# Making the last chunk of five output blocks in the middle of the sixth block's chunks

## The reference

```python
z = h @ w_in                                   # h = modulated rmsnorm(x)
att = neighbourhood attention(q, k, v, context keys and values)   # 512 features
sg, cv = gated parts of z                                         # 256 + 256 features
y = concat([att, sg, cv]) @ w_out              # 1024 x 1024, the first output product
x = x + mod[2] * y                             # mod: six vectors of c @ ada_w + ada_b
h2 = rmsnorm(x, norm2_g) * (1 + mod[4]) + mod[3]
x = x + mod[5] * conv_ffn(h2)
```

## Time and profile before

| | |
|---|---|
| median of 3 runs | 1409.8 us (1407.17 to 1410.17) |
| the profiled execution's own time | 1409.92 us |
| its span | 1408.6 us |
| TensorE busy (matmuls) | 1365.2 us, 97% of the span |
| VectorE busy | 757.5 us, 54% |
| ScalarE busy | 605.3 us, 43% |
| mean granted clock of TensorE | 0.990 |

### The profile page before, as it was taken

How to read it: one execution, slowest core, us unless ns; L and a number is a source line. 1 busy time by engine, 2 the same in 40 slices (tenths; PEclk the granted TensorE clock), 3 DMA queues, 4 the chain that set the end, 5 groups by cost and what they waited for, 6 DMA issues and landing times.

```text
span 1408.6 us, 17387 instructions
## 1 busy us (share of the span) xinstructions
PE 1365.2 (97%) x7040; PEld 1129.4 (80%) x7040; DVE 757.5 (54%) x1070; ACT 605.3 (43%) x866; POOL 4.0 (0%) x11
## 2 busy tenths in 40 slices
PE   5999997999999999999999999999999999999997
PEld 4777776788888888888888888788997888888887
DVE  5678855575555443335524444345777666564224
ACT  5646866453333333223334545334524443443221
POOL 0000000000000000000000000000000000000000
PEclk9999999999999999999999999999999999999999
DMA  9743321323432323323232121234402323323331
GB/s 379 279 140 136 124 72 59 127 76 135 149 135 90 105 86 98 95 82 104 70 110 71 64 75 45 76 95 143 137 1 77 103 90 105 104 86 98 95 95 60
DMA packets 43102, 150.45 MB, mean 107 GB/s; under 512 B 4752, under 2 KB 6928, under 8 KB 41872
## 3 DMA queue, kind: packets, MB, share of 16 engines
q1 hardware_dynamic: 42144, 144.76, 31.1%
q0 software_dynamic: 880, 4.59, 1.0%
HBM read 146.45 MB, written 2.10 MB: 105 GB/s over the span
## 4 chain that ended last, share of the span: by engine, by line
PE 88%; DVE 6%; ACT 3%; issue 2%; DMA 1%; DVEq 0%; SPq 0%; ACTq 0%
PE banks L578 26%; PE banks L579 26%; PE banks L580 26%; ACT w_hi L1315 1%; PE banks L719 1%; DVE w_lo L1864 1%; PE banks L730 1%; PE banks L722 1%; PE banks L1125 1%; PE banks L1124 1%; PE banks L863 1%; PE banks L1116 1%; PE banks L1152 1%; PE banks L846 1%; PE banks L692 1%
## 5 line engine op out<-in xcount | busy, mean ns | idle before, releaser
L578 PE MATMUL banks<-h_lo,w_hi 128*128 128x512 f32 (+1 forms) x1248 | 475.3, 381 | 6.7 <-DVE h_lo L2203 2.1
L579 PE MATMUL banks<-h_hi,w_lo 128*128 128x512 f32 (+1 forms) x1248 | 471.5, 378 | 0.0
L580 PE MATMUL banks<-h_hi,w_hi 128*128 128x512 f32 (+1 forms) x1248 | 470.0, 377 | 0.0
L1864 DVE TENSOR_TENSOR w_lo<-raw_w,w_hi 128x1024 fp32r<-128x1024 f32 (+2 forms) x221 | 256.1, 1161 | 323.9 <-ACT w_hi L1315 321.6
L1315 ACT ACTIVATE w_hi<-raw_w 128x1024 fp32r<-128x1024 f32 (+2 forms) x221 | 221.6, 1005 | 236.8 <-PE banks L580 210.6
L578 PEld LDWEIGHTS banks<-h_lo,w_hi 128*128 128x128 f32 x1248 | 236.2, 189 | 58.5 <-issue 7.4
L580 PEld LDWEIGHTS banks<-h_hi,w_hi 128*128 128x128 f32 x1248 | 236.2, 189 | 43.5
L579 PEld LDWEIGHTS banks<-h_hi,w_lo 128*128 128x128 f32 x1248 | 236.4, 189 | 41.7
L578 PE MATMUL banks<-a_lo,w_hi 128*128 128x512 f32 (+1 forms) x396 | 146.2, 369 | 0.0
L579 PE MATMUL banks<-a_hi,w_lo 128*128 128x512 f32 (+1 forms) x396 | 146.2, 369 | 0.0
L580 PE MATMUL banks<-a_hi,w_hi 128*128 128x512 f32 (+1 forms) x396 | 145.3, 367 | 0.0
(11 more groups left out here) (314 smaller groups left out, 1517.9 us busy)
## 6 DMA issues: line engine op xcount, KB each, us to landing
raw_w<-in_w_ffn_up SPq DMA_DIRECT2D x44, 512.0 KB, 3.3
raw_w<-in_w_up SPq DMA_DIRECT2D x44, 512.0 KB, 3.4
raw_w<-in_ada_rows SPq DMA_DIRECT2D x24, 512.0 KB, 4.0
early<-in_ada_turned SPq DMA_DIRECT2D x8, 1024.0 KB, 17.2
raw_w<-in_w_gates SPq DMA_DIRECT2D x16, 512.0 KB, 3.3
raw_w<-in_w_ffn_down SPq DMA_DIRECT2D x16, 448.0 KB, 3.3
raw_w<-in_w_down SPq DMA_DIRECT2D x16, 448.0 KB, 3.4
raw_w<-in_w_conv SPq DMA_DIRECT2D x12, 512.0 KB, 3.2
```

What stands on the lines that cost most here:

```text
L578: e.matmul(dst, lhs_hi, rhs_lo, start=first, stop=False)
L579: e.matmul(dst, lhs_lo, rhs_hi, start=False, stop=False)
L580: return e.matmul(dst, lhs_hi, rhs_hi, start=False, stop=last)
L1864: e.tensor_tensor(lo[:, 0:n], raw[:, i % RAW, 0:n], hi[:, 0:n].bitcast(F32), ALU.subtract).then_inc(s_lo, 1)
```

## The change

Four things are done. (1) The tile "last" is loaded before "full0", so "last" is tile 25 and "full0" tile 26. (2) TensorE makes four chunks of block 5, then the eighth chunk of blocks 0 to 4, then the last four chunks of block 5. `freed[0]` is now given after them, and the count in it is 11, since block 5 is added into x last. (3) VectorE adds blocks 0 to 4 first and block 5 after them; the sums of squares lag by one block. The split of "full1"'s first tile, which VectorE did as the last thing of output block 4 in the mixer, is done after `attended_lo`; rows 22 and 23 of `ada_w` are asked for in the step of block 3. (4) `modulation_ready(3, 2)` and the vector `gain` stand ahead of the additions instead of behind them. ScalarE's squares follow the new order of blocks.

```diff
--- before.py
+++ after.py
@@ -132,10 +132,10 @@
     for o in range(OUT_SPLIT):
         l.tile("out", io["w_out"][o, :, 0:KC - 1, :], (KC - 1) * P, 0, KC - 1)
         l.row()
+    l.tile("last", io["w_out_last"][:, :], OUT_SPLIT * P, 0, OUT_SPLIT)
     l.block("full0", "w_out", OUT_SPLIT)
     while l.n_rows < ROWS_BEFORE_NORM2:
         l.row()
-    l.tile("last", io["w_out_last"][:, :], OUT_SPLIT * P, 0, OUT_SPLIT)
     for o in range(OUT_SPLIT + 1, KC):
         l.block("full1", "w_out", o)
     for f in range(FC):
@@ -532,7 +532,7 @@
         HALF = T // 2
         HALVES = [slice(0, HALF), slice(HALF, T)]
         NT = TT // 2
-        FINAL_ORDER = (OUT_SPLIT, *range(OUT_SPLIT))
+        FULL_BEFORE_LAST = 4
         ADA_BANKS = (4, 5, 4, NORM_BANKS[0])
         LATE_BANKS = (1, 2, 3, 4, 5)
         LAST_TWO = (OUT_SPLIT + 1, OUT_SPLIT + 2)
@@ -947,16 +947,19 @@
 
 
 
-            for j in range(KC):
+            for j in range(FULL_BEFORE_LAST):
                 out_product(OUT_SPLIT, W["full0"], j, 0, KC)
-            freed[0] = (s_x1, OUT_SPLIT + 1)
             for o in range(OUT_SPLIT):
                 hi, lo = tile_of(W["last"])
                 b, w, k = LATE_BANKS[o], slice(o * P, (o + 1) * P), OUT_ORDER[KC - 1]
                 free(b)
+                e.wait_ge(s_mix_lo, KC)
                 done = product(bank[b][:, :], hi[:, w], lo[:, w], h_hi[:, k, :], h_lo[:, k, :], True, True)
                 done.then_inc(s_late if o < OUT_SPLIT - 1 else s_used, 1)
-                freed[b] = (s_x1, OUT_SPLIT + 2 + o)
+                freed[b] = (s_x1, OUT_SPLIT + 1 + o)
+            for j in range(FULL_BEFORE_LAST, KC):
+                out_product(OUT_SPLIT, W["full0"], j, 0, KC)
+            freed[0] = (s_x1, 2 * OUT_SPLIT + 1)
 
             def second_sum(half):
                 b, tok = NORM_BANKS[half], HALVES[half]
@@ -1559,11 +1562,11 @@
                 e.activation(h_hi[:, k, HALVES[half]], piece(half, k), ACT.Identity,
                              bias=mod[:, 3 * KC + k:3 * KC + k + 1]).then_inc(h_two.hi.sem, 1)
 
-            prepare(W["full0"] + 3)
+            prepare(W["last"] + 3)
             e.preload_act_table(ACT.Sqrt)
-            for n, o in enumerate(FINAL_ORDER):
-                x1_square(n, OUT_SPLIT + n + 1, x[:, o, :], squares[:, (n - 1) % 2, :] if n else exact[:, 0, :])
-                if n == 0:
+            for o in range(OUT_SPLIT + 1):
+                x1_square(o, OUT_SPLIT + o + 1, x[:, o, :], squares[:, (o - 1) % 2, :] if o else exact[:, 0, :])
+                if o == 1:
                     prepare(W["full1"] + 2)
             prepare(W["up"] + 1)
             for n, o in enumerate(LAST_TWO):
@@ -2165,7 +2168,10 @@
                         e.wait_ge(s_mod, 1)
                         e.wait_ge(s_used, t + 1)
                         add_gated(b, o, 2 * KC, s_x1)
-                        after_tile(t)
+                        if o < OUT_SPLIT - 1:
+                            after_tile(t)
+                        if o == OUT_SPLIT - 2:
+                            rows(loads.tile_load[W["full1"]])
 
 
 
@@ -2204,9 +2210,11 @@
                                        in1=h_hi[:, k, tok].bitcast(F32), op0=ALU.add, op1=ALU.subtract).then_inc(h_two.lo.sem, 1)
 
             every = slice(0, T)
-            e.wait_ge(s_used, W["full0"] + 1)
-            add_gated(0, OUT_SPLIT, 2 * KC, s_x1, every)
             low(W["full1"] + 1)
+            modulation_ready(3, 2)
+            e.wait_ge(s_mod, 2)
+            e.scalar_tensor_tensor(out=gain[:, :], in0=mod[:, 4 * KC:5 * KC], scalar=1.0, in1=cols_of("norm2_g"), op0=ALU.add,
+                                   op1=ALU.mult).then_inc(s_mod, 1)
             for o in range(OUT_SPLIT):
                 if o < OUT_SPLIT - 1:
                     e.wait_ge(s_late, o + 1)
@@ -2214,15 +2222,14 @@
                     e.wait_ge(s_used, W["last"] + 1)
                 e.wait_ge(s_x1, o + 1)
                 add_gated(LATE_BANKS[o], o, 2 * KC, s_x1, every)
-                if o == 0:
+                if o >= 2:
+                    add_squares(o - 1, every, o % 2, o)
+                if o == 2:
                     low(W["full1"] + 2)
-                else:
-                    add_squares(o, every, (o - 1) % 2, o + 1)
+            add_squares(OUT_SPLIT - 1, every, OUT_SPLIT % 2, OUT_SPLIT)
+            e.wait_ge(s_used, W["full0"] + 1)
+            add_gated(0, OUT_SPLIT, 2 * KC, s_x1, every)
             add_squares(OUT_SPLIT, every, (OUT_SPLIT - 1) % 2, OUT_SPLIT + 1)
-            modulation_ready(3, 2)
-            e.wait_ge(s_mod, 2)
-            e.scalar_tensor_tensor(out=gain[:, :], in0=mod[:, 4 * KC:5 * KC], scalar=1.0, in1=cols_of("norm2_g"), op0=ALU.add,
-                                   op1=ALU.mult).then_inc(s_mod, 1)
             add_last_two(0, 0)
             add_squares(KC - 2, HALVES[0], 1, KC - 1)
             add_last_two(1, 0)
```

## The result

The changed kernel took 1412.34 us in the median of 20 runs (1410.37 to 1415.26), the kernel before 1409.57 us in the median of 20 runs beside it (1407.17 to 1411.97). The ratio is 1.0023, 95% interval 1.0016 to 1.003: slower by some 3 us, and clear of none. Which of "same" (48%) and "slower by over 0.2%" (45%) came true isn't decided: by the ratio it is slower by a hair, by the bound of 1412.6 us the median lies just under it, and the interval reaches to both sides. "Faster" (7%) didn't come true.

What follows compares the result with a forecast made beforehand. TensorE, busy 97% of the span, was taken as the bound, so only its idle time and clock count. Terms -0.73 + 3.87 - 1.79 + 1.4 - 0.2 = +2.55 us on 1409.92 gave 1412.5 us; range 1410.3 to 1414.3.

Steps and rivals of the forecast that it cites:

- same: Outcome for the whole kernel: a change of under 0.2%, not to be told from none; chance 48%.
- slower by over 0.2%: Outcome for the whole kernel: a time above 1412.6 us; chance 45%.
- the bound of 1412.6 us: Kernel time that separates "same" from slower, a change of 0.2% or 2.8 us.
- Faster: Outcome for the whole kernel: a shorter time than the kernel before; chance 7%.
- Part a: Transposes near 253 us: the small tile first shortens the copy and split ahead of them, gaining 0.73 us.
- Part b: TensorE from block 5 to "full1": still the same 13 chunks of 0.69 us, now ending at 272.63.
- Part c: Bank 0 before block 6: a new wait of 3.87 us for block 5's addition, last in VectorE's queue.
- Part d: First sum of squares (L654): its wait goes, 1.79 us won; the sum comes 1.35 us later, before any clock cost.
- Part e: Behind the wait at bank 0: TensorE's clock falls, costing 1.4 us, bounds 0.8 and 2.4.
- Brings a fall nearly surely: Claim that a TensorE wait of 3.9 us is almost certainly followed by a fall of the clock.
- The gain of 0.2: Feed-forward's start, behind the sum: VectorE's addition at 288.88 no longer waits for TensorE; 0.2 us won, bounds 0 and 0.3.
- The wait of 2.1 us: TensorE's wait in the feed-forward's first tiles, counted as fixed, with the clock's fall behind it.

Runs made afterwards that it cites:

- 10: Kernel before with bank 7 instead of bank 0 for the first half of block 6, nothing else: 1408.0 us, ratio 1.0001.
- 5: The changed kernel once more, unedited, as measure for runs beside it on the same chip: 1412.02 us, ratio 1.0019 to the kernel before.
- 7: Changed kernel with copy and split of the small tile "last" made 1024 columns wide instead of 640: 1413.34 us, ratio 1.0032 to the kernel before.
- 12: Changed kernel with the factors' two instructions (`modulation_ready(3, 2)`, `gain`) put back behind the additions: 1411.6 us, ratio 1.0024 to the kernel before.
- 3: Changed kernel with 15 needless 512-wide matmuls into bank 7 inside the wait at bank 0: 1412.1 us, ratio 1.002 to the kernel before.
- 6: Changed kernel with 15 needless matmuls in the wait at bank 0, measured once more: 1411.82 us, ratio 1.0022 to the kernel before.
- 2: Kernel before, but TensorE opens bank 0 for block 6 only after ten additions, which it doesn't need: 1413.19 us, ratio 1.0027.
- 11: Kernel before with the needless wait for ten additions at bank 0, filled with 15 needless matmuls into bank 7: 1411.79 us, ratio 1.0023.
- 1: Changed kernel with the first half of block 6 in bank 7 instead of bank 0: 1408.07 us, ratio 0.9991 to the kernel before.
- 4: Changed kernel with VectorE adding block 5 right behind the second "full1" tile's split, ahead of blocks 3 and 4: 1408.19 us, ratio 0.9991.
- 8: Changed kernel with bank 7, the first half's last high parts before table load and weight copy, last low part before its split: 1406.63 us, ratio 0.9985.
- 9: Changed kernel with bank 7, last high and low parts moved ahead, and ScalarE's table load behind all high parts: 1404.78 us, ratio 0.9976.

## Why the prediction was right, and where it was not

Distances in the profiled executions, from the third block's addition, and the low clock between the wait and the sum:

| execution | to the first sum | to the end | low clock there |
|---|---|---|---|
| kernel before | 33.08 | 1159.05 | none |
| 10, its bank alone | 33.09 | 1157.47 | none |
| changed kernel | 36.41 | 1162.02 | 3.4 us |
| 5, once more | 37.31 | 1160.80 | 6.8 us, partly in the wait |
| 7, wide tile | 38.05 | 1161.44 | 6.8 us, partly in the wait |
| 12, factors late | 34.62 | 1159.56 | none |
| 3 and 6, filler | 34.89, 34.90 | 1160.03, 1160.19 | none |
| 2, wait alone | 36.89 | 1160.14 | 3.4 us |
| 11, wait alone, filler | 35.10 | 1160.67 | none |
| 1, other bank | 31.08 | 1156.26 | none |
| 4, block 5 sooner | 32.03 | 1156.33 | none |
| 8, next wait | 31.06 | 1157.16 | none |
| 9, table load later | 31.05 | 1153.08 | none |

**Part a** held. Block 5 begins at 263.91, 14.03 us behind the third block's addition; before, it began at 264.30, 14.75 behind its own, so 0.72 is gained of 0.73. Run 7 gives it back, 0.74. `attended_lo` ended at 265.37, 1.4 us before the first eighth chunk (266.78), and no wait for it arose.

**Part b** held: from 263.91 to the last matmul's start at 272.73 plus 0.23 are 9.05 us, 13 chunks.

**Part c** held almost to the number: TensorE could have gone on at 272.96 and did at 276.91, 3.95 us against 3.87. Bank (run 1) and queue order (run 4) each remove or shrink it alone, and the wait put into the old kernel brings the loss (run 2). This is shown, not only argued. The rule of the Trainium skill on rotating banks ("Perfetto Trace Analysis", section "Matmuls") agrees with run 1: with another bank the wait of 3.95 us is gone.

**Part d** held: no wait at L654. VectorE's last total ahead of the sum ended at 285.76, 0.5 us before the sum began.

**Part e** is the term that was mis-sized: its size isn't fixed. I took 1.4 with bounds 0.8 and 2.4. From opening bank 0 to the sum took 9.38 us in the changed kernel's profile, 10.28 in run 5 (277.23 to 287.51) and 7.57 in run 12, against the 7.48 of an undisturbed stretch: 1.9, 2.8 and 0.1, for the same wait in nearly the same code. Two of the three lie outside my bounds. Not all of it is the fall: runs 3, 4 and 6, without one, took 7.85, so that the fall itself cost 1.5 in the changed kernel's profile and 2.4 in run 5. "Brings a fall nearly surely" was wrong: of five profiled executions with such a wait (these three and runs 2 and 7) one had none. The same holds for the shorter wait at L654: a fall behind it in the kernel before, none in run 10.

What a fall costs at the sum is not what it costs at the end, for later falls come or stay away. The executions with a filler (3, 6 and 11) had a fall in the feed-forward's first tiles and two more between 1000 and 1040 us; runs 2 and 5 had only the last of these three. So the 1.5 to 2.4 us by which runs 3 and 6 had the sum sooner became 0.6 to 2.0 at the end, and the 1.8 of run 11 became a loss of 0.5. Run 12, without fall and filler, ended 0.5 us sooner than runs 3 and 6.

The record has the mean granted clock of every timed run. One fall of 3.4 us at half the clock takes 0.0012 off it (3.4 / 2 / 1411). It is 0.9907 for the changed kernel and 0.9911 for run 5, and 0.9907 for both runs 3 and 6, means whose errors are 0.0002 to 0.0005: on the whole the filler took no low clock out of an execution. So the runs with and without it, though they lie within 0.2 us of each other, don't price a fall. What does bear on the price are the 93 runs of the kernel before that stand beside runs 1 to 12: on each of the three chips the executions with a lower mean clock took longer, by 0.8 us per 0.001, which makes 1.0 us for a fall, an estimate from a correlation. With 1.0 in place of 1.4 the sum would have given 1412.1. How many falls the change adds in the timed runs isn't shown: against the kernel before beside it, run 5's mean clock is 0.0003 lower and run 12's 0.0012. And one profile of each says little about the end: the kernel before and run 10 do the same work and their profiled ends lie 1.6 us apart. So the wait, its length and its cause were foreseen, while the agreement within 0.2 us is in part luck.

**The gain of 0.2** was 0.29: from the first sum to the second 9.49 us before and 9.20 in the changed kernel (36.41 to 45.61). Run 10, with the wait at L654 but no fall behind it, took 9.27, so some 0.2 of it is the fall that went away, as the term had it. The other 0.07 goes with the wait itself: 9.27 to 9.29 in the runs that wait at the first sum (1, 8, 9 and 10), 9.19 to 9.21 in the changed kernel and all other runs. The wait of 2.1 us stayed as counted. Three short waits for `h_lo` ahead of it are new (0.80, 0.21 and 0.15 us, which make the total 3.3 instead of 2.1); run 10 has them too, so they go with the full clock there and not with the change.

Not tried: the swap of the two tiles alone under the old order of chunks. Tile 25's slot would be written again while its user had not come yet, so the copy's wait would have to change as well, and the run would test two things.

## What to carry to other kernels

When a piece of work is moved later in an order, look for the buffer that it fills and ask who opens that buffer next: here a group moved to the end of its stage filled the very bank with which the next stage began, and its release had moved to the end of another engine's queue. The length of such a wait can be read beforehand, instruction by instruction, from the consumer's queue in the old trace (3.87 worked out, 3.95 measured). A saving at a wait on the path is worth what the next wait leaves of it. The repair was cheap here: another bank, or one addition earlier in the queue. And needless work that keeps the clock up at one place is to be judged by the whole execution: here falls came at other places, and the mean clock stayed as it was.

## What was not expected of the hardware

- The clock behind a wait of TensorE of 3.8 us stayed full in one execution, fell for 3.4 us in another and for 6.8 us in a third. Later falls came and went as well: at 1014.6 us the kernel before has one, though the profile shows no wait of TensorE from 985 us up to it, and run 5 at the same work has none. The rows, kernel before first, then run 5:

```profile
1014.60:1018.10 3.50, 3.50 (x19) 3.50 (x19) 1.78 (x9) 1.32 (x4) 0.00 (x0) 0.51 0.02 5
```

```profile
1015.60:1019.10 3.50, 3.50 (x33) 3.50 (x32) 0.66 (x5) 0.26 (x1) 0.00 (x0) 1.00 0.02 5
```

- Half-wide matmuls (256 columns) at the full clock start either 0.113 us apart, as in the earlier trace rows, or 0.118, as in the changed kernel from 280.64 to 286.17 (47 steps). Run 12 has 0.113 behind the same wait; run 11 has 0.113 too, runs 3, 4 and 6 have 0.118. Over the 66 matmuls of 22 chunks that is 0.3 us. I found no cause.
